# The third query chunk of the first tile moved ahead of the first expert sum on TensorE, and the fourth put beside the first four picks

## Chip, cores and metric

One NeuronCore of a Trainium2 chip runs the whole program. The metric is device time in microseconds, lower is better. All data are float32.

## What is computed

Two transformer blocks on 256 tokens of width 2048. The first block mixes by attention and retention and then applies a layer with 16384 experts, of which each token picks 16 for each of 8 heads. The part that matters here, cut from the reference:

```python
def peer(x, w_query, sub_keys, expert_down, expert_up):
    qry = (xt @ w_query).reshape(T, H, 2, PEER_HALF_DIM)          # 2048 -> 2048
    s = jnp.einsum('thpd,phnd->thpn', qry, sub_keys)               # scores of the keys
    top_s, top_i = lax.top_k(s, K)
    ...
    best_s, best_pos = lax.top_k(cand_s.reshape(T, H, K * K), K)
    expert_idx = jnp.take_along_axis(cand_i.reshape(T, H, K * K), best_pos, axis=-1)
    gates = jax.nn.softmax(best_s, axis=-1)
    ...
        u = expert_down[ib]                                        # 128 experts of each token
        act = jax.nn.gelu(jnp.einsum('td,thkd->thk', xb, u), approximate=False)
        vv = expert_up[ib]
        return jnp.einsum('thk,thkd->td', gb * act, vv)
```

The second block has forgetting attention, a recurrent branch, and 32 dense experts in four groups.

## The kernel before

The tokens are two tiles of 128 (`T2 = 2`). The first tile goes ahead: its projections, attention, retention and output product run alone up to about 500 us. Then the expert layer of the first block begins, in **picks**: `n` of 0 to 127 is the first tile, 128 to 255 the second, and pick `n` is the n-th chosen expert of each of the 128 tokens. For each pick

- GpSimd issues two indirect gathers, in program order: the down row of 128 tokens (128 x 2048 f32, 1 MB) into a ring of three places (`DOWN_ROWS`), freed by the dot product of pick n-3, and the up row of the same size into a ring of three places, four from pick 12 on, freed when its earlier row has been added. The fourth place for the first tile is `XT[:, 0]`, the first tile's turned activations; it is free when the last unit of the fourth query chunk has been used (L881);
- VectorE takes the dot product of the down row with the normed activations (L2561);
- ScalarE applies gelu and gate, and writes a diagonal matrix (L1937 to L1945);
- TensorE adds the up row by four matmuls with that diagonal (L1497, the "sum" of the pick) into banks 0 to 3. Where `n % 4 == 3` VectorE adds it instead (L2412), after the dot product of pick n+1.

The indices come from `choose(g)` on VectorE, 32 picks at a time. `choose(g)` needs the key scores of head pair g, that is chunk g of the query product. `choose(0)` runs whole before pick 0; `choose(1)` is spread over picks 0 on, `choose(2)` over 32 on, `choose(3)` over 64 on, and `choose(4)`, the first of the second tile, starts at the pick `FIFTH`.

The query product of the first tile has four chunks of 512 columns. Chunk `c` is four **units** (`query_unit(c, j)`, two for chunk 0), each with a weight load of its own and 4 matmuls of 128 x 512 (L946). A chunk goes to bank 4 or 5 in turn, is kept by ScalarE (`keep_query`), turned (L952), kept, and multiplied with the keys (`key_scores`, L1068).

Weights are loaded by SyncE in a fixed order of units. From the second query chunk on a unit is 1 MB and lies in a ring of four places; a load waits until the unit four ahead of it has been used.

Beside the picks run the rest of the second tile's first block (units `in1` for its projections, then `gate_a`, `gate_r`, `att`, `ret`, `mix`, `query`), and from pick 129 on the second block of the first tile. `steps_beside_picks()` writes this order by hand: tables with **ticks**, one tick for each pick, and for each engine which steps come after that pick's own work. Each engine runs its table in order. The first lines build the query steps and set the tick `at = x + 4` from which all the second tile's steps follow; the second block's starts are constants (134 and 261).

Of the kernel before, what the change touches and what calls it, by code (L numbers as in the profile page):

```python
# [131 lines left out]
def steps_beside_picks():  # L132

    pe, act, dve = {}, {}, {}

    def put(table, tick, *step):
        table.setdefault(tick, []).append(step)

    when = {}
    for i in range(8):  # L140
        key = ("query", 0, 2 + i // 4, i % 4)
        when[key] = int(i * 1.15)
        put(pe, when[key], *key)
    for c in (2, 3):
        x = when["query", 0, c, 3]
        put(act, x + 1, "query", 0, c)
# [200 lines left out]
def two_blocks(nc, A, consts, out):  # L347
    f32, u32 = mybir.dt.float32, mybir.dt.uint32
    ALU, ACT, AX = mybir.AluOpType, mybir.ActivationFunctionType, mybir.AxisListType.X
    AFTER1 = steps_of_first_block()  # L350
    BESIDE_PE, BESIDE_ACT, BESIDE_DVE, FIFTH, TICKS = steps_beside_picks()
    ds = bass.ds

    ctx = ExitStack()
    with ctx:
# [218 lines left out]
        def slot(i, n=CH):  # L574

            _, lo, hi = PLACES[i]
            return W[:, :, :].rearrange("p s n -> p (s n)")[:, lo:hi].rearrange("p (k n) -> p k n", n=n)

        def depth(key):

            _, lo, hi = PLACES[INDEX[key]]
            return (hi - lo) // columns(key)
# [67 lines left out]
        def query_out(t, c):  # L650

            return bank[4 + (c if t else c % 2)]
# [5 lines left out]
        def keys_out(t, c):  # L658

            return bank[4 + c if t else 7]  # L660
# [247 lines left out]
        def _(pe):  # L908
            turns = 0

            def xt(k, t):
                return XT[:, t, k * P:(k + 1) * P]
# [27 lines left out]
            def unit(key, out, lhs, first, last):  # L940

                i = INDEX[key]
                pe.wait_ge(w_loaded[SLOT[i]], LANDED[i])
                ks = depth(key)
                for k in range(ks):
                    mm = pe.matmul(out, lhs(k), slot(i)[:, k, :], start=first and k == 0, stop=last and k == ks - 1)  # L946
                mm.then_inc(w_used, 1)
# [91 lines left out]
            def query_unit(c, j):  # L1039

                if j == 0 and c >= 2:
                    pe.wait_ge(query_kept, c - 1)
                elif j == 0:
                    pe.wait_ge(mixed, 4)
                    pe.wait_ge(merged_kept, 4)
                if c == 0:
                    pe.wait_ge(kept1, 2 + 2 * j)
                ks = 4 if c else 8
                unit(("query", 0, c, j), query_out(0, c)[:, :], lambda k: xt(ks * j + k, 0), j == 0, ks * j + ks == KC)

            def turn_query(t, c):

                pe.wait_ge(query_kept, 4 * t + c + 1)
                if t == 0 and c:
                    pe.wait_ge(qt_kept, c)
                elif t == 0:
                    pe.wait_ge(kept1, 4)
                turn_four(qt_out(t, c), QN[:, c % 2, :]).then_inc(query_turned, 1)

            def key_scores(t, c):  # L1060

                pe.wait_ge(qt_kept, 4 * t + c + 1)
                pe.wait_ge(keys_kept, 4)
                if t == 0 and c:
                    pe.wait_ge(s_kept, c)
                for j in range(4):
                    b = 4 * c + j
                    mm = pe.matmul(keys_out(t, c)[:, j * P:(j + 1) * P], QT[:, c % 2, j * P:(j + 1) * P],  # L1068
                                   KT[:, (b % 2) * 8 + b // 2, :], start=True, stop=True)
                mm.then_inc(peer_scored, 1)  # L1070
# [281 lines left out]
            for c in range(2):  # L1352
                for j in range(4 if c else 2):
                    query_unit(c, j)
                turn_query(0, c)
                key_scores(0, c)

            def turn2(t, c):

                pe.wait_ge(x2_ready, t + 1)  # L1360
                if t == 1:
                    pe.wait_ge(out2_added, 4)
                    pe.wait_ge(attn_kept, 6)
                turn_four(bank[c], H[:, t, c * CH:(c + 1) * CH]).then_inc(turned2, 1)
# [303 lines left out]
        def _(act):  # L1668
# [84 lines left out]
            def exps(n):  # L1753
                _, _, _, _, sm, _ = att(n)
                _, _, nk = group(n)
                act.wait_ge(scores_ready, n + 1)
                for hh in range(4):
                    act.activation(sm[:, hh, 0:nk], sm[:, hh, 0:nk], ACT.Exp, bias=nmx[:, hh:hh + 1],
                                   accum_out=rs[:, hh:hh + 1]).then_inc(exp_ready, 1)
                if n < 4:  # L1760
                    act.activation(es, es, ACT.Exp).then_inc(exp_ready, 1)
                else:
                    act.activation(es, nmx, ACT.Copy).then_inc(exp_ready, 1)
# [1103 lines left out]
```

## Time and profile before

| | |
|---|---|
| median of 3 runs | 3296.32 us (3295.13 to 3297.55) |
| profiled execution, time | 3301.08 us |
| profiled execution, span | 3299.3 us |
| TensorE busy | 2946.0 us (89%) |
| VectorE busy | 1237.3 us (38%) |
| ScalarE busy | 545.2 us (17%) |
| GpSimd busy | 705.8 us (21%) |
| moved by DMA | 1206.78 MB, mean 366 GB/s |

The time of the profiled execution is 1.8 us above its span. Busy time is a sum over stages that differ in what limits them; the rows below keep them apart.

### The profile page before, as it was taken

How to read it: one execution, taken by the hardware profiler on the slowest of the kernel's cores; microseconds unless marked ns; L12 is line 12 of the kernel's file. 1: busy time of each engine (PE TensorE's matmuls, PEld its weight loads, DVE VectorE, ACT ScalarE, POOL GpSimd, SP SyncE). 2: the span in 40 equal slices, each digit the busy share in tenths (PEclk: the TensorE clock that was granted, in tenths of full speed). 3: DMA queues.
4: the chain of work that ended last, by engine and by line, in shares of the span. 5: the costliest groups of instructions: out<-in, count | busy, mean ns of one | idle time of the engine just before them, and what ended most of it. 6: DMA issues, size and time to landing. Idle time of an engine off the chain costs nothing.

```text
span 3299.3 us, 23959 instructions
## 1 busy us (share of the span) xinstructions
PE 2946.0 (89%) x8013; PEld 1300.7 (39%) x8013; DVE 1237.3 (38%) x1894; ACT 545.2 (17%) x1292; POOL 705.8 (21%) x598
## 2 busy tenths in 40 slices
PE   8999998799889999897687877877799999999999
PEld 4444443344444434343333333333254433333344
DVE  1100005535354443335755655554522123322220
ACT  1111001112121110112213211211122111001010
POOL 1000002323233222324534443434300000000000
PEclk9999999999999999998898989898899999999999
DMA  9878887999999999999999999999977759999972
GB/s 352 300 279 289 301 301 295 417 412 410 412 374 417 421 422 421 421 421 417 408 419 372 417 418 419 419 419 420 374 249 259 259 208 422 422 422 422 422 302 76
DMA packets 268049, 1206.78 MB, mean 366 GB/s; under 512 B 16640, under 2 KB 19248, under 8 KB 164656
## 3 DMA queue, kind: packets, MB, share of 16 engines
q1 hardware_dynamic: 193600, 668.09, 52.4%
q0 software_dynamic: 74352, 537.48, 39.6%
q8 instruction: 51, 0.84, 0.1%
q14 instruction: 46, 0.38, 0.0%
HBM read 1203.41 MB, written 2.10 MB: 365 GB/s over the span
## 4 chain that ended last, share of the span: by engine, by line
PE 46%; DMA 40%; DVE 4%; issue 4%; DVEq 2%; ACT 2%; POOL 1%; SPq 1%; ACTq 0%; POOLq 0%
DMA W<-in_peer_expert_down,big 26%; PE bank L946 14%; DMA W<-in_w_expert_up 8%; PE bank L936 6%; PE bank L1497 6%; PE bank L1108 5%; PE bank L1604 4%; PE bank L1662 3%; DMA W<-in_w_in 3%; DVE W L2561 2%; DVEq L2411 1%; DMA XT<-in_peer_expert_up,big 1%; PE bank L1013 1%; PE bank L1372 1%; DMA W<-in_w_peer_query 1%
## 5 line engine op out<-in xcount | busy, mean ns | idle before, releaser
L2561 DVE CUSTOM_DVE_ANT_0 W<-W,big 128x2048 f32<-128x2048 f32 x256 | 586.1, 2291 | 695.8 <-DMA W<-in_peer_expert_down,big 694.5
L874 POOL DMA_INDIRECT W<-in_peer_expert_down,big x256 | 349.2, 1364 | 1228.0 <-DVE small L2561 629.1
L1497 PE MATMUL bank<-XT,big 128*128 128x512 f32 x488 | 300.3, 773 | 205.2 <-ACT big L1945 178.6
L946 PE MATMUL bank<-W,XT 128*128 128x512 f32 x704 | 308.6, 596 | 3.3 <-DMA W<-in_w_peer_query 3.3
L1497 PE MATMUL bank<-XS,big 128*128 128x512 f32 x536 | 249.8, 610 | 34.0 <-ACT big L1945 26.4
L1497 PEld LDWEIGHTS bank<-XT,big 128*128 128x128 f32 x488 | 119.2, 254 | 374.4 <-issue 244.4
L1497 PE MATMUL bank<-W,big 128*128 128x512 f32 x512 | 238.1, 609 | 26.9 <-ACT big L1945 21.1
L1937 ACT ACTIVATE small<-small 128x1 f32<-128x1 f32 x256 | 51.8, 202 | 1227.6 <-DVE small L2561 1222.0
L1604 PE MATMUL bank<-W,XS 128*64 128x512 f32 x1024 | 226.7, 596 | 14.3 <-DMA W<-in_w_expert_up 11.7
L1108 PE MATMUL bank<-W,XT 128*128 128x512 f32 x480 | 217.1, 602 | 21.3 <-DMA W<-in_w_in 19.1
L936 PE MATMUL bank<-W,XT 128*128 128x512 f32 x480 | 211.9, 599 | 3.0 <-DMA W<-in_w_in 3.0
L946 PEld LDWEIGHTS bank<-W,XT 128*128 128x128 f32 x704 | 133.5, 191 | 166.3 <-issue 161.2
L883 POOL DMA_INDIRECT XS<-in_peer_expert_up,big x130 | 163.0, 1254 | 161.3 <-PE bank L1497 121.2
L946 PE MATMUL bank<-W,big 128*128 128x512 f32 x448 | 194.4, 593 | 1.0 <-ACT big L1725 1.0
L1013 PE MATMUL bank<-W,XT 128*128 128x512 f32 x384 | 170.0, 597 | 2.0 <-DVE XT L2093 2.0
L1497 PEld LDWEIGHTS bank<-XS,big 128*128 128x128 f32 x536 | 101.1, 194 | 172.4 <-issue 149.5
L1497 PEld LDWEIGHTS bank<-W,big 128*128 128x128 f32 x512 | 98.5, 196 | 151.8 <-issue 143.5
L899 POOL COPY XS<-XT 128x448 f32 x32 | 17.0, 561 | 654.5 <-issue 369.8
L2412 DVE SCALAR_TENSOR_TENSOR H<-XS,small,H 128x2048 f32<-128x2048 f32 x63 | 148.1, 2351 | 12.3 <-ACT small L1939 6.6
L1108 PEld LDWEIGHTS bank<-W,XT 128*128 128x128 f32 x480 | 90.9, 192 | 138.5 <-issue 110.4
L1372 PE MATMUL bank<-W,XT 128*128 128x512 f32 x320 | 143.8, 592 | 0.0
L1604 PEld LDWEIGHTS bank<-W,XS 128*64 128x64 f32 x1024 | 78.7, 138 | 159.8 <-issue 159.8
(376 smaller groups left out, 2690.9 us busy)
## 6 DMA issues: line engine op xcount, KB each, us to landing
W<-in_w_in SPq DMA_DIRECT2D x66, 2048.0 KB
W<-in_w_in SPq DMA_DIRECT2D x132, 1024.0 KB
W<-in_w_expert_gate SPq DMA_DIRECT2D x68, 1024.0 KB, 15.0
W<-in_w_expert_up SPq DMA_DIRECT2D x68, 1024.0 KB, 17.0
big<-in_w_expert_down SPq DMA_DIRECT2D x32, 2048.0 KB, 12.6
W<-in_w_out SPq DMA_DIRECT2D x16, 2048.0 KB
W<-in_w_out SPq DMA_DIRECT2D x32, 1024.0 KB
W<-in_w_peer_query SPq DMA_DIRECT2D x28, 1024.0 KB
```

Of the source, the lines that this page charges most:

```text
L874: pool.indirect_dma_start(down_row(n), None, down_t, row).then_inc(down_in[n % DOWN_ROWS], 16)
L883: pool.indirect_dma_start(up_row(n), None, up_t, row).then_inc(up_in[b], 16)
L936: mm = pe.matmul(bank[q % 4][:, :], xt(8 * half + k, 0), slot(u)[:, k, :], start=half == 0 and k == 0, stop=half == 1 and k == 7)
L946: mm = pe.matmul(out, lhs(k), slot(i)[:, k, :], start=first and k == 0, stop=last and k == ks - 1)
L1013: mm = pe.matmul(bank[4 + c][:, :], lhs, slot(i, D)[:, 0, c * CH:(c + 1) * CH], start=first, stop=last)
L1108: mm = pe.matmul(bank[4 + c][:, :], xt(ks * j + k, 1), slot(i, width)[:, k, c * CH:(c + 1) * CH], start=j == 0 and k == 0, stop=ks * j + k ...
L1372: mm = pe.matmul(bank[c][:, :], lhs(k), slot(i, 1024)[:, k, c * CH:(c + 1) * CH], start=first and k == 0, stop=last and k == 1)
L1497: mm = pe.matmul(bank[4 * (n // P) + c][:, :], DIAG[:, m % 4, :], up_row(n)[:, c * CH:(c + 1) * CH], start=n % P == 0, stop=n % P == P - 2)
L1604: mm = pe.matmul(bank[2][lo:hi, :], XTE[:, p, 8 * half + k, lo:hi], moving(half, e, k), start=half == 0 and k == 0, stop=half == 1 and k == 7)
L1662: mm = pe.matmul(bank[2 * (n % 2) + t][:, :], xt(8 * j + k, t), slot(u)[:, k, :], start=j == 0 and k == 0, stop=j == 1 and k == 7)
L2412: STT(h, up_row(n), wts[:, j:j + 1], h, ALU.mult, ALU.add).then_inc(added_dve, 1)
L2561: dve.tensor_tensor_reduce(out=down_row(n), in0=down_row(n), in1=HN[n // P], scale=1.0, scalar=0.0, op0=ALU.mult, op1=ALU.add, accum_out=d ...
```

## The change

The query units of the third chunk (`c = 2`) are written ahead of the loop over the picks, right behind the key scores of the second chunk, so they precede the first sum. The units of the fourth chunk (`c = 3`) go to ticks 0, 1, 2 and 3. Before, the eight units had the ticks 0, 1, 2, 3, 4, 5, 6 and 8.

```diff
     when = {}
-    for i in range(8):
-        key = ("query", 0, 2 + i // 4, i % 4)
-        when[key] = int(i * 1.15)
-        put(pe, when[key], *key)
+    for j in range(4):
+        when["query", 0, 2, j] = -1
+        when["query", 0, 3, j] = j
+        put(pe, j, "query", 0, 3, j)
     for c in (2, 3):
         x = when["query", 0, c, 3]
         put(act, x + 1, "query", 0, c)
...
                 turn_query(0, c)
                 key_scores(0, c)
+            for j in range(4):
+                query_unit(2, j)
```

The loop below takes its ticks from `x`. The third chunk's keep, turn and key scores move from ticks 4 to 7 to ticks 0 to 3, the fourth's from 9 to 12 to 4 to 7. `at` becomes 7 instead of 12, and with it every step of the second tile's first block stands 5 ticks earlier, and `FIFTH` is 111 instead of 116. The order of SyncE's loads and of GpSimd's gathers is the same.

TensorE's order of before, from the second query chunk to the fifth sum. L946 from `W,XT` is query units (4 matmuls each), L952 turning, L1068 key scores, L1497 the sum of a pick:

```order
L946 MATMUL bank<-W,XT 128x512 x16
L952 MATMUL bank<-C,big 128x128 x4
L1068 MATMUL bank<-big 128x128 x4
L1497 MATMUL bank<-W,big 128x512 x4
L946 MATMUL bank<-W,XT 128x512 x4
L1497 MATMUL bank<-XS,big 128x512 x4
L946 MATMUL bank<-W,XT 128x512 x4
L1497 MATMUL bank<-XS,big 128x512 x4
L946 MATMUL bank<-W,XT 128x512 x8
L1497 MATMUL bank<-XS,big 128x512 x4
L946 MATMUL bank<-W,XT 128x512 x4
L1497 MATMUL bank<-XS,big 128x512 x4
```

The same place with the change (the sum's line is now L1499):

```order
L946 MATMUL bank<-W,XT 128x512 x16
L952 MATMUL bank<-C,big 128x128 x4
L1068 MATMUL bank<-big 128x128 x4
L946 MATMUL bank<-W,XT 128x512 x16
L1499 MATMUL bank<-W,big 128x512 x4
L946 MATMUL bank<-W,XT 128x512 x4
L1499 MATMUL bank<-XS,big 128x512 x4
L946 MATMUL bank<-W,XT 128x512 x4
L952 MATMUL bank<-C,big 128x128 x4
L1499 MATMUL bank<-XS,big 128x512 x4
L946 MATMUL bank<-W,XT 128x512 x4
L1068 MATMUL bank<-big 128x128 x4
```

Sixteen matmuls have gone from between the sums to a place ahead of the first.

VectorE's order of before at the normalization of the second tile's retention. L2561 is a pick's dot product (the second row of each pair reads out its sum), L2412 an addition of an up row, L2217 to L2226 the normalization, L2400 and L2402 the end of `choose(2)`:

```order
L2561 ISA W,small<-W,big 128x2048
L2561 ISA small 128x1
L2400 RECIPROCAL small<-small 128x2
L2402 TENSOR_TENSOR big<-big,small 128x32
L2561 ISA W,small<-W,big 128x2048
L2561 ISA small 128x1
L2217 RECIPROCAL small<-small 128x8
L2222 TENSOR_SCALAR big<-big,small 128x256 x8
L2226 TENSOR_TENSOR big<-big 128x2048
L2561 ISA W,small<-W,big 128x2048
L2561 ISA small 128x1
L2412 SCALAR_TENSOR_TENSOR H<-XS,small,H 128x2048
```

The same with the change (line numbers two higher):

```order
L2563 ISA W,small<-W,big 128x2048
L2563 ISA small 128x1
L2386 TENSOR_TENSOR big<-big,C 128x512
L2219 RECIPROCAL small<-small 128x8
L2224 TENSOR_SCALAR big<-big,small 128x256 x8
L2228 TENSOR_TENSOR big<-big 128x2048
L2563 ISA W,small<-W,big 128x2048
L2563 ISA small 128x1
L2389 TENSOR_TENSOR big<-big 128x512
L2563 ISA W,small<-W,big 128x2048
L2563 ISA small 128x1
L2414 SCALAR_TENSOR_TENSOR H<-XS,small,H 128x2048
```

The normalization now stands between steps of `choose(2)`, and one more dot product lies between it and the next addition.

## Rows read from the trace of the kernel before

**Rows 1.** The page: span, bus rate in 40 slices, chain by engine.

```profile
span 3299.3 us, 23959 instructions
...
GB/s 352 300 279 289 301 301 295 417 412 410 412 374 417 421 422 421 421 421 417 408 419 372 417 418 419 419 419 420 374 249 259 259 208 422 422 422 422 422 302 76
...
PE 46%; DMA 40%; DVE 4%; issue 4%; DVEq 2%; ACT 2%; POOL 1%; SPq 1%; ACTq 0%; POOLq 0%
```

**Rows 2.** Busy time by stage, granted clock, DMA share, rate.

```profile
core 0: us, PE busy (x) PEld busy (x) DVE busy (x) ACT busy (x) POOL busy (x), PEclk, DMA share, GB/s
...
530.00:1500.00 970.00, 878.68 (x2126) 395.46 (x2127) 415.93 (x543) 158.98 (x419) 291.12 (x230) 0.96 1.01 412
1500.00:2380.00 880.00, 676.21 (x1525) 297.67 (x1524) 519.43 (x693) 198.22 (x531) 366.93 (x282) 0.88 1.01 413
```

**Rows 3.** Timeline of TensorE: start, duration, group [idle time before it, releaser].

```profile
514.02 13.90 PE L946 MATMUL bank<-W,XT 128*128 128x512 f32 x32
...
529.95 1.16 PE L1068 MATMUL bank<-big 128*128 128x128 f32 x8 [0.69 <-ACT big L1865]
542.74 6.46 PE L1497 MATMUL bank<-W,big 128*128 128x512 f32 x8 [11.64 <-ACT big L1945]
549.05 3.60 PE L946 MATMUL bank<-W,XT 128*128 128x512 f32 x8
552.48 3.60 PE L1497 MATMUL bank<-XS,big 128*128 128x512 f32 x8
...
600.73 3.70 PE L946 MATMUL bank<-W,XT 128*128 128x512 f32 x8 [1.93 <-DMA W<-in_w_peer_query]
```

**Rows 4.** Timeline of VectorE: the indices, the first dot product.

```profile
531.20 0.19 DVE L2393 SCALAR_TENSOR_TENSOR big<-big 128x32 uint32<-128x32 f32 x1
...
537.89 2.29 DVE L2561 CUSTOM_DVE_ANT_0 W<-W,big 128x2048 f32<-128x2048 f32 x1 [3.80 <-DMA W<-in_peer_expert_down,big]
```

**Rows 5.** Timeline of GpSimd: the first gather, the seventh and the eighth.

```profile
532.41 1.04 POOL L874 DMA_INDIRECT W<-in_peer_expert_down,big  x1 [453.95 <-issue]
...
541.30 0.94 POOL L874 DMA_INDIRECT W<-in_peer_expert_down,big  x1 [0.30 <-issue]
550.02 2.77 POOL L883 DMA_INDIRECT W<-in_peer_expert_up,big  x1 [7.79 <-PE bank L1497]
```

**Rows 6.** Slices of 2 us, columns as in rows 2.

```profile
532.00:534.00 2.00, 0.00 (x0) 0.00 (x0) 0.45 (x3) 1.36 (x2) 1.28 (x2) 1.00 0.18 70
534.00:536.00 2.00, 0.00 (x0) 0.00 (x0) 0.09 (x1) 0.00 (x0) 1.67 (x2) 0.68 0.91 262
536.00:538.00 2.00, 0.00 (x0) 0.00 (x0) 0.11 (x1) 0.00 (x0) 1.41 (x2) 0.50 0.97 377
...
552.00:554.00 2.00, 2.00 (x6) 0.95 (x5) 1.14 (x8) 0.90 (x3) 1.70 (x2) 1.00 0.83 217
554.00:556.00 2.00, 2.00 (x6) 0.85 (x5) 1.35 (x1) 0.00 (x0) 0.03 (x1) 1.00 0.79 307
```

**Rows 7.** A slice of a stretch with gathers alone.

```profile
1580.00:1600.00 20.00, 11.88 (x24) 4.78 (x23) 10.56 (x12) 2.50 (x9) 8.97 (x8) 0.83 1.01 420
```

**Rows 8.** Timeline of VectorE: its wait for the inner products.

```profile
906.26 0.69 DVE L2200 TENSOR_TENSOR big<-bank,C 128x512 f32<-128x512 f32 x1 [25.86 <-PE bank L1141]
```

**Rows 9.** Slices of 20 us, columns as in rows 2.

```profile
900.00:920.00 20.00, 20.00 (x54) 9.44 (x53) 6.30 (x9) 4.19 (x8) 5.68 (x4) 1.00 0.85 317
920.00:940.00 20.00, 17.79 (x50) 9.18 (x49) 12.56 (x14) 7.50 (x15) 8.74 (x4) 1.00 0.91 361
...
980.00:1000.00 20.00, 11.20 (x29) 5.30 (x29) 14.98 (x19) 8.83 (x20) 11.72 (x8) 0.83 0.96 365
...
1040.00:1060.00 20.00, 20.00 (x48) 8.93 (x47) 4.60 (x4) 1.80 (x6) 2.81 (x3) 1.00 1.02 423
...
1800.00:1820.00 20.00, 15.24 (x31) 6.66 (x32) 19.31 (x43) 6.79 (x14) 9.88 (x6) 0.83 0.77 287
```

**Rows 10.** The dot products: duration min/median/max, first and last start.

```profile
L2561 DVE CUSTOM_DVE_ANT_0 W<-W,big x256: 2258/2292/2348, 537.9 to 2383.8; 128x2048 f32<-128x2048 f32 x128
```

## The prediction

> **What bounds the kernel now.** I read the page first, then the stage table, the timeline around the first pick on TensorE, VectorE and GpSimd, the same stretch in slices of 2 us, and the places where the DMA engines were not full.
>
> The page [rows 1] shows where TensorE and the DMA engines meet: in the chain, TensorE has 46% and DMA 40%, and the rate on the bus jumps from about 300 GB/s to above 410 in the eighth slice, where the picks begin. The stage table [rows 2] gives the split. From 530 to 1500 us (picks 0 to about 111, with the second tile's weights beside them) the DMA moved 412 GB/s, its share reads 1.01, while TensorE was busy 878.68 of 970 us, 91%. From 1500 to 2380 us it is the same with TensorE at 676.21 of 880. After 2380 us no pick is left, and the change does not touch that part. So the stretch in which the change acts runs at the rate of the DMA engines. TensorE comes second, close behind: it has 9% of slack up to 1500 us.
>
> Around the first pick [rows 3] the reader is to see one hole. TensorE ends the key scores of the second query chunk at 531.1 us and starts the first sum at 542.74, 11.64 us later. The chain across that hole is serial [rows 4, 5]: VectorE writes the indices at 531.20, GpSimd issues the first gather at 532.41, the first dot product starts at 537.89, ScalarE makes the diagonal, and TensorE sums. And the first sum is slow: 6.46 us for the same four matmuls that take 3.60 a few us later [rows 3]. The granted clock in 534 to 536 us is 0.68 [rows 6], and 0.50, the 1.2 GHz level, in the slice behind it.
>
> **What the change does to TensorE at the hole.** It puts the four units of the third query chunk (16 matmuls) where TensorE was idle. The second chunk, the same 16 matmuls, took 13.90 us [rows 3]. From 531.1 us that ends at 545.0, which is 2.3 us after the old start of the first sum. But TensorE has then not been idle, so I take the sum at 3.60 us instead of 6.46: it ends at 548.6 instead of 549.2. So the first sum ends no later, and 13.9 us of matmuls are already done. If TensorE set the pace afterwards, the change would be worth 13.9 + 0.6 = 14.5 us. The cost of this edit on the first picks is thus about nothing. If the clock stayed at the lower level the sum would end at 545.0 + 6.46 = 551.5 us, 2.3 us late; the cover for this is that the next gather into the up ring waits for that sum [rows 5], and the seven gathers ahead of it are 7.3 MB, 17.6 us at full rate from about 534 us, so the engines are fed until then.
>
> The Trainium skill, TensorE: Matmul & The Clock Gate (Part 1: The HAM clock gate), says the same of the mechanism: the default is the throttled clock, and activity releases it. By it too the first sum would run at full clock; the sum is the same without it.
>
> **What it does to the DMA engines.** The bytes are the same, in the same order in SyncE's queue. What can be gained is time in which the engines now lie idle and would have something to load. The units live in a ring of four places of 1 MB, so the loads of the fourth chunk wait for the units of the third to be used. Before, the first of these is used up at 552.6 us [rows 3]; now, at 3.5 us a unit, at 534.6, 538.1, 541.5 and 545.0. So four loads of 1 MB are asked for 18 us or more earlier. From 532 to 556 us [rows 6] the slices that fall short of the 418 GB/s of a full one are:
> - 532 to 534 us, 70 GB/s: too early, the first new load is asked for at 534.6 us. Gain nothing.
> - 534 to 536 us, 262 GB/s: the gathers are just starting. The missing (418-262)/418 x 2 = 0.7 us may be half filled. 0.4 us.
> - 552 to 554 us, 217 GB/s and 554 to 556 us, 307 GB/s: GpSimd waited 7.79 us until 550.02 with the fourth up gather, and in program order the next down gather stands behind it [rows 5]. A weight load fills this now: (201+111)/418 x 2 = 1.5 us.
> Together 1.9 us. Elsewhere the new loads only take bandwidth from gathers that the same engines carry. The second and third down rows land later, by up to 4.2 MB / 418 GB/s = 10 us, and this is given back when those bytes are no longer due. The 13.9 us that TensorE has won turns into waits for rows and weights.
>
> The Trainium skill, DMA: Bandwidth & Descriptors (Issuing engines are not separate DMA queues), states the rule that speaks against a larger gain: transfers of SyncE and GpSimd run on the same 16 engines and interleave. [rows 2] with 1.01 at 412 GB/s agree with it. By it the 14.5 us are not to be had while the engines are full.
>
> **What moves with it.** The third chunk no longer takes ticks 0 to 3, the fourth takes 0 to 3 instead of 4 to 8, and the table derives every later step of the second tile from that. So turns, key scores, all `in1` units, attention, retention and the six wide products stand 5 picks earlier, beside GpSimd's queue, which is unchanged; SyncE's queue is in the same order too. The steps of the second block (from tick 129) stay. So five gather-only picks move from ahead of the `in1` units to behind the last query unit. A gather-only stretch is at full rate too, 420 GB/s at 1580 to 1600 us [rows 7]: cost nothing. The first gather into the place freed by the fourth chunk's last unit (pick 12) comes after it with more room. The other 3 up places have to do for picks 7 to 11 beside two units each; by count, a pick there moves 4.2 MB, 10 us, so the ring covers 30 us. A row needs some 14 of them: 5.5 from the issue to the dot product, 2.3 for that, 2.6 for the diagonal, 3.6 for the sum [rows 3 to 5]. Nothing.
>
> What I can't price is the alignment. Of four picks, one is added by VectorE, not TensorE, and its addition stands behind the next dot product. A shift by 5 moves every step by one against that pattern, and against VectorE's choosing of the next indices (ticks 32 to 50). That matters where VectorE, in order, waits for TensorE: at 906.26 us it had waited 25.86 us for the inner products [rows 8], and queued behind that are the dot products, for which the down gathers wait. DMA then fell to 317 and 361 GB/s at 900 to 940 us and to 365 at 980 to 1000 [rows 9], against 423 in full flow. By 418 GB/s that is 4.8, 2.7 and 2.5 us, 10.0 in all, in the steps from the first inner products to the normalization. Bounds: all of it goes (-10.0), or as much again is added (+10.0). The same waits exist after as before, with three of their four TensorE ticks holding a sum in both. I take 0.
>
> **The sum.** The profiled execution has a span of 3299.3 us and a time of 3301.08. 3301.08 - 1.9 = 3299.2. The median of the runs is 4.76 us below the profiled execution, so on their scale 3296.32 - 1.9 = 3294.4 us. I take 3294.5.
>
> **The rivals.**
> - TensorE sets the pace. For it: TensorE at 20.00 us of 20 at 1040 to 1060 [rows 9], and 91% over the stretch. Against it: in the same row the DMA engines are full. All 14.5 us would give 3281.8. It needs the DMA engines to find 14 us of idle time up to tick 50; there are the 1.9 and the 10.0.
> - The shift, with TensorE 13.9 us ahead, closes the holes at 900 to 1000 us. 1.9 + 10.0 = 11.9 us: 3284.4. Half of it, 6.9 us, is at the edge of what can be told. For it: the normalization now stands one dot product away from VectorE's addition instead of right ahead of it. Against: TensorE's lead is spent at the start, since it waits there for the same bytes.
> - A new hole, slower. One VectorE wait of the attention or retention falls together with an addition or a choosing step, the down gathers stop, and four weight places can't keep the engines full. How deep such a hole can be shows 1800 to 1820 us, 287 GB/s, which is 6.3 us lost [rows 9]; with a repeat as at 900 to 940 it is 10. Then 3294.4 + 10.0 = 3304.4. It decides (slower by over 0.2%) once new holes exceed 6.6 + 1.9 = 8.5 us.
> - The change does nothing: the third chunk's own loads are late and TensorE waits all the same. The load of its last unit can start when the second chunk's last unit is used up, at 527.9 us [rows 3]; 1 MB at full rate is 2.5 us, and even at twice that it is there before 541.5, when TensorE comes to it. I give this no separate time; it is within the forecast.
>
> **How the numbers follow.** A measurement of this kernel tells 0.2%, 6.6 us, from no change. Forecast (3294.4, with alignment within +-5 us): 0.55. Holes closed, by more than half: 0.24. TensorE's pace: 0.05. New holes: 0.16, of which some 0.12 pass the bound. Faster by over 0.2%: 0.24 + 0.05 less a little that falls short, 0.27. Slower: 0.12 and 0.03 for what I haven't thought of, 0.15. Same: 0.58. The range is to leave 2 in 10 out: from the closed holes (3284.4) with 1 us to spare, to just below the new hole's end, 3303. TensorE's pace lies outside. The forecast's own range is 3289 to 3300.
>
> **What would show each step.** Right: no idle time of 11 us ahead of the first sum, its four matmuls in 3.6 us, its end near 548.6 us; the slices at 552 to 556 us full; the fourth chunk's last unit done near 570 us instead of 604 [rows 3]; the picks' last dot product (now 2383.8 us by its start [rows 10]) earlier by only about 2 us. Wrong: a last dot product earlier by over 7 us, with the slices at 900 to 1000 us near 418 GB/s; or a new row of under 350 GB/s between 600 and 1000 us, and VectorE waiting over 20 us for TensorE beside it.

## The result, and the profile after

The changed kernel takes 3304.55 us (median, 3300.32 to 3307.93) against 3296.42 for the kernel before on the same chip (3293.69 to 3299.04): ratio 1.0021, 95% interval [1.0012, 1.0029]. It is slower, and above the range, whose upper end was 3303. The ratio here and below is the record's estimate from all single runs with its interval; it is not the quotient of the two medians, which would be 1.0025. In microseconds the loss is 6.9 [4.0, 9.6] by the ratio and 8.1 by the medians.

The page of the changed kernel (span, bus rate in 40 slices, chain by engine), which answers to [rows 1]:

```profile
span 3302.5 us, 23959 instructions
...
GB/s 353 302 275 293 301 295 307 414 382 402 415 387 422 421 421 421 421 421 414 420 419 360 417 419 419 418 419 419 376 238 268 261 205 422 421 422 422 422 304 76
...
PE 48%; DMA 38%; DVE 4%; issue 4%; DVEq 3%; ACT 1%; SPq 1%; POOL 1%; ACTq 0%; POOLq 0%
```

The eighth slice, where the picks begin, is 414 against 417; the ninth (660 to 743 us) has fallen from 412 to 382, and the tenth (743 to 826 us) from 410 to 402. Start and end of the dot products, as [rows 10]:

```profile
L2563 DVE CUSTOM_DVE_ANT_0 W<-W,big x256: 2258/2292/2327, 537.5 to 2386.4; 128x2048 f32<-128x2048 f32 x128
```

The picks end 2.6 us later than in [rows 10], although the execution profiled there was 4.8 us above its median and this one lies on it. So the two traces show 2.6 us of a loss of 7 to 8, and I read places from them, not the sum.

TensorE at the first sums (columns as in [rows 3]):

```profile
530.39 13.90 PE L946 MATMUL bank<-W,XT 128*128 128x512 f32 x32
544.12 3.60 PE L1499 MATMUL bank<-W,big 128*128 128x512 f32 x8
550.79 3.67 PE L946 MATMUL bank<-W,XT 128*128 128x512 f32 x8 [3.07 <-DMA W<-in_w_peer_query]
554.30 3.60 PE L1499 MATMUL bank<-XS,big 128*128 128x512 f32 x8
562.76 5.40 PE L946 MATMUL bank<-W,XT 128*128 128x512 f32 x8 [4.87 <-DMA W<-in_w_peer_query]
...
576.20 3.60 PE L946 MATMUL bank<-W,XT 128*128 128x512 f32 x8
```

The idle 11.64 us are filled, the first sum takes 3.60 us and ends at 547.7. The third chunk did what it was to do. The slices (columns as in [rows 2]):

```profile
552.00:554.00 2.00, 2.00 (x6) 0.89 (x5) 1.91 (x4) 0.20 (x1) 0.00 (x0) 1.00 1.01 410
554.00:556.00 2.00, 2.00 (x6) 0.82 (x5) 0.97 (x7) 0.70 (x2) 0.00 (x0) 1.00 1.02 413
640.00:660.00 20.00, 10.37 (x15) 4.24 (x16) 7.57 (x9) 0.90 (x3) 2.98 (x1) 0.74 1.03 405
660.00:680.00 20.00, 20.00 (x48) 8.92 (x47) 6.68 (x11) 1.48 (x4) 5.91 (x4) 1.00 0.90 333
680.00:700.00 20.00, 20.00 (x55) 9.37 (x55) 8.10 (x10) 4.22 (x14) 6.05 (x4) 1.00 0.97 368
780.00:800.00 20.00, 20.00 (x59) 9.77 (x58) 8.48 (x11) 3.34 (x10) 3.30 (x3) 1.00 0.90 357
```

The two slices of [rows 6] that fell short are full. But there is a new hole at 660 to 700 us, and a smaller one at 780 to 800 us (357, where the kernel before has 417), to which the section on the units comes back. Of the first, the order is the thing to see: from 640 to 660 the DMA engines are full and TensorE works 10.37 us of 20; then TensorE works 20.00 of 20 and the DMA engines fall to 333. Each in turn waits for the other. TensorE ahead of the hole:

```profile
623.90 3.60 PE L1499 MATMUL bank<-XS,big 128*128 128x512 f32 x8
627.34 3.60 PE L1108 MATMUL bank<-W,XT 128*128 128x512 f32 x8
632.69 3.70 PE L1108 MATMUL bank<-W,XT 128*128 128x512 f32 x8 [1.76 <-DMA W<-in_w_in]
644.63 5.64 PE L1108 MATMUL bank<-W,XT 128*128 128x512 f32 x8 [8.24 <-DMA W<-in_w_in]
655.27 5.40 PE L1108 MATMUL bank<-W,XT 128*128 128x512 f32 x8 [5.00 <-DMA W<-in_w_in]
660.50 3.60 PE L1499 MATMUL bank<-XT,big 128*128 128x512 f32 x8
```

VectorE and GpSimd behind it:

```profile
671.79 0.29 DVE L2120 TENSOR_TENSOR big<-big,C 128x128 f32<-128x128 f32 x1 [23.93 <-ACT big L1745]
```

```profile
664.91 0.94 POOL L883 DMA_INDIRECT XT<-in_peer_expert_up,big  x1 [17.03 <-PE bank L1499]
675.21 1.35 POOL L883 DMA_INDIRECT W<-in_peer_expert_up,big  x1 [8.12 <-PE bank L1499]
```

The rows at 644.63 and 655.27 are units 8 and 9 of `in1`, the first two of group 1 (keys and values of the second tile's attention). TensorE waited 8.24 and 5.00 us for their weights. Pick 11 has no sum on TensorE, so the sum of pick 12 stands behind both, at 660.50, and GpSimd, in program order, gathered nothing for 17.03 us.

### The profile page after: what moved, and what is told of

It is laid out like the page before. It is cut to its first block, busy times and chain, and to the rows that moved or that the text cites. A ratio compares the mean times of both kernels' runs of the same rounds, so it can differ in the third digit from the quotient of the medians.

```text
span 3302.5 us, 23959 instructions
## 1 busy us (share of the span) xinstructions
PE 2953.6 (89%) x8013; PEld 1304.5 (40%) x8013; DVE 1236.1 (37%) x1894; ACT 545.0 (17%) x1292; POOL 709.4 (21%) x598
## 4 chain that ended last, share of the span: by engine, by line
PE 48%; DMA 38%; DVE 4%; issue 4%; DVEq 3%; ACT 1%; SPq 1%; POOL 1%; ACTq 0%; POOLq 0%
DMA W<-in_peer_expert_down,big 26%; PE bank L946 14%; DMA W<-in_w_expert_up 8%; PE bank L1499 7%; PE bank L936 5%; PE bank L1108 5%; PE bank L1606 4%; PE bank L1664 3%; DMA W<-in_w_in 3%; DVEq L2413 2%; PE bank L1013 1%; DVE W L2563 1%; PE bank L1374 1%; PE bank L1590 1%; DMA XT<-in_peer_expert_up,big 1%
## 5 line engine op out<-in xcount | busy, mean ns | idle before, releaser
L1499 PE MATMUL bank<-XT,big 128*128 128x512 f32 x488 | 312.7, 800 | 210.8 <-ACT big L1947 177.3
L946 PE MATMUL bank<-W,XT 128*128 128x512 f32 x704 | 309.9, 598 | 7.9 <-DMA W<-in_w_peer_query 7.9
L1499 PEld LDWEIGHTS bank<-XT,big 128*128 128x128 f32 x488 | 122.4, 261 | 385.1 <-issue 278.1
L1499 PE MATMUL bank<-XS,big 128*128 128x512 f32 x536 | 244.6, 600 | 23.9 <-ACT big L1947 21.2
L1499 PE MATMUL bank<-W,big 128*128 128x512 f32 x512 | 236.6, 606 | 22.1 <-DMA W<-in_peer_expert_up,big 13.2
L1606 PE MATMUL bank<-W,XS 128*64 128x512 f32 x1024 | 225.4, 593 | 14.1 <-DMA W<-in_w_expert_up 11.5
L946 PEld LDWEIGHTS bank<-W,XT 128*128 128x128 f32 x704 | 133.9, 192 | 171.0 <-issue 164.6
L946 PE MATMUL bank<-W,big 128*128 128x512 f32 x448 | 194.4, 593 | 1.0 <-ACT big L1727 1.0
L1499 PEld LDWEIGHTS bank<-XS,big 128*128 128x128 f32 x536 | 99.2, 191 | 154.4 <-issue 140.9
L1499 PEld LDWEIGHTS bank<-W,big 128*128 128x128 f32 x512 | 98.3, 194 | 149.2 <-issue 129.2
## 6 DMA issues: line engine op xcount, KB each, us to landing
W<-in_w_out SPq DMA_DIRECT2D x32, 1024.0 KB, 11.5
```

What stands on the lines that cost most here:

```text
L1499: mm = pe.matmul(bank[4 * (n // P) + c][:, :], DIAG[:, m % 4, :], up_row(n)[:, c * CH:(c + 1) * CH], start=n % P == 0, stop=n % P == P - 2)
L1606: mm = pe.matmul(bank[2][lo:hi, :], XTE[:, p, 8 * half + k, lo:hi], moving(half, e, k), start=half == 0 and k == 0, stop=half == 1 and k == 7)
```

## What the experiments tell apart

All ratios are to the kernel before, run on the same chip as the experiment (its median was 3297.37, 3298.62, 3297.85, 3297.65 and 3298.99 us in the five sets), five rounds each, and hold 95% intervals. Where a run is "the changed kernel with", the rest is as in the diff.

### The query chunks, or the shift

Two theories. *Chunks*: the earlier query loads beside the first gathers cost. *Shift*: the second tile's steps at tick 7 in place of 12 cost.

```diff
-    at = x + 4
+    at = 12        # e1;  at = 8 in e2
```

> Both query chunks as in the change (third ahead of the first sum, fourth at ticks 0 to 3), but every later step of the second tile back at its old tick (at = 12 instead of 7). Theory shift: the loss comes from the second tile's steps standing 5 ticks earlier; then this is level with the kernel before or up to 2 us faster, ratio 0.9990 to 1.0005. Rival chunks: the loss comes from the query weights that are loaded beside the first gathers; then this is as slow as the change, ratio about 1.002.

e1: 3298.96 us, 1.0003 [0.9994, 1.0012].

> The change with the second tile's steps moved by 4 ticks instead of 5 (at = 8), so that every step stands at the old place in the pattern of four picks. Theory parity (a kind of shift): the place among the four picks decides; then this is within 2 us of the kernel before. Theory ring: what costs is units of the second tile beside picks that still have three up places (before pick 12); then this is slow like the change, ratio about 1.002.

e2: 3297.59 us, 1.0002 [0.9993, 1.0011].

In e4 the third chunk alone goes ahead of the first sum, and the fourth has the ticks 4, 5, 6 and 8, so that nothing is shifted:

> Only the third chunk goes ahead of the first sum; the fourth stays at ticks 4, 5, 6 and 8 and the second tile's steps stay where they were (at = 12). Theory shift: level or up to 2 us faster, ratio 0.9990 to 1.0005. Rival chunks: slower, about half or all of the loss, ratio 1.001 to 1.002.

e4: 3296.82 us, 0.9997 [0.9988, 1.0006].

*Chunks* falls: without the shift, one chunk moved (e4) or both (e1) make no difference that can be told. The loss belongs to the shift. But a shift of four ticks (e2) costs nothing and one of five 2.1 thousandths, so it is not how early the steps are. The ticks between, `at = 9` (e6), `10` (e8) and `11` (e5):

> The second tile's steps moved by 3 ticks (at = 9). Theory parity (only a start one tick ahead of a multiple of four is bad): level, 0.9995 to 1.0005. Rival early: level too. A ratio over 1.001 speaks against both.

> The second tile's steps moved by 2 ticks (at = 10). Theory parity: level, 0.9995 to 1.0005. Rival early: level. With the other starts this completes the scan from 7 to 12.

> The change with the second tile's steps moved by 1 tick instead of 5 (at = 11, which has the same remainder by 4 as the change's 7). Theory parity: a hole of 5 to 7 us at the first two rotations as in the change, ratio about 1.0015. Rival early: only the start at 7 is too early, and this is level with the kernel before, 0.9995 to 1.0005.

Measured: 1.0000 [0.9991, 1.0009] at 9 (3298.80), 1.0025 [1.0014, 1.0035] at 10 (3307.47), 1.0025 [1.0016, 1.0034] at 11 (3307.73). Tick 11 came as *parity* had it. Tick 10 did not: level was expected, by both theories, so a start one tick ahead of a multiple of four is not the only bad one.

### The place against VectorE's picks

VectorE adds the picks with remainder 3 by 4. If the distance from these counts, then moving the pattern must undo the loss of the changed kernel (e9), and can bring one on the kernel before (e10):

```diff
-BY_DVE = [n for n in range(PICKS) if n % 4 == 3]
-BY_PE = [n for n in range(PICKS) if n % 4 != 3]
+BY_DVE = [n for n in range(PICKS) if n % 4 == (2 if n < 60 else 3)]   # 1 in e10
+BY_PE = [n for n in range(PICKS) if n not in BY_DVE]
```

> The change as it is, with all ticks kept, but for picks below 60 VectorE adds those with remainder 2 by 4 instead of 3. The four narrow units (the 512 key and value columns, 2 KB rows) stand at ticks 11 and 12; the pick without a sum on TensorE is then 10 instead of 11. Theory pattern: a narrow unit on a tick without a sum is what costs; back to the kernel before, ratio 0.9990 to 1.0007, hole at 620 to 700 us under 3 us. Rival place: the absolute tick of the steps decides (against the choosing of indices, or the up ring); still 1.0015 to 1.0025.

Measured 3294.73, 0.9989 [0.9980, 0.9998], the lowest ratio of all.

> The kernel before with no part of the change; for picks below 60 VectorE adds those with remainder 1 instead of 3. Its narrow units stand at ticks 16 and 17, and pick 17 is now without a sum on TensorE. Theory pattern: slower than before, ratio 1.001 to 1.0025, with a hole of 4 us or more at 640 to 720 us. Rival place: level, 0.9995 to 1.0005.

Measured 3301.72, 1.0010 [0.9999, 1.0020]: in the direction expected, at the edge of the interval. The control, remainder 2 on the kernel before:

> The kernel before with VectorE adding picks 2, 6, 10 ... 58 in place of 3, 7, 11 ... 59; the second tile's steps stay at tick 12. Theory 'distance to VectorE's picks': the steps' start less the remainder is 10, 2 by modulo 4, one of the level distances, so 0.999 to 1.000 (3296). If remainder 2 is better by itself, whatever the distance, then this is as fast as the changed kernel with it: 0.999 or below.

Measured 3296.48, 0.9998 [0.9989, 1.0007]. The table is by distance (tick of the second tile's first unit less the remainder, modulo 4). It has TensorE's waits for all `in1` weights from 590 to 700 us and the mean rate from 530 to 1020 us. "Narrow pair" is the time in which the 1024 pieces of 2 KB of units 8 and 9 were moved, counted by size from the packets of each trace. The next column is the lowest of the three slices of 20 us from 780 to 840 us. Both are taken up below.

| kernel | tick, remainder | distance | waits, us | GB/s | narrow pair, us | lowest, 780 to 840 | ratio |
|---|---|---|---|---|---|---|---|
| before | 12, 3 | 1 | 5.9 | 403 | 11.5 | 412 | 1 |
| e1 | 12, 3 | 1 | 5.1 | 403 | 10.3 | 413 | 1.0003 |
| e4 | 12, 3 | 1 | 4.9 | 406 | 13.0 | 414 | 0.9997 |
| e2 | 8, 3 | 1 | 6.0 | 405 | 10.5 | 410 | 1.0002 |
| e9 | 7, 2 | 1 | 9.9 | 407 | 13.0 | 415 | 0.9989 |
| e6 | 9, 3 | 2 | 8.3 | 406 | 12.1 | 394 | 1.0000 |
| e16 | 12, 2 | 2 | 6.6 | 409 | 10.2 | 392 | 0.9998 |
| e8 | 10, 3 | 3 | 11.4 | 396 | 13.5 | 265 | 1.0025 |
| e10 | 12, 1 | 3 | 7.5 | 402 | 12.1 | 335 | 1.0010 |
| after | 7, 3 | 0 | 15.0 | 400 | 19.5 | 357 | 1.0021 |
| e5 | 11, 3 | 0 | 15.2 | 399 | 22.3 | 374 | 1.0025 |

The rule by distance was written down in this form only ahead of e16. e9's own expectation was narrower: a narrow unit on a tick without a sum on TensorE costs. At distance 0 units 8 and 9 stand on such a tick (11 in the changed kernel, 15 at tick 11). At distance 1 it is units 6 and 7, whose pieces are wide, and most of the waits of the table are for these. (So of the waits that e17's expectation gives for the kernel before, 2.08 and 3.48 us are for units 6 and 7; only 0.33 is for a narrow one. The 1.44 us of e18's is also for unit 7.)

### What makes the hole: the ring, the hold, the order

A "hold" is VectorE standing, in program order, at a step that waits for another engine, with dot products behind it.

The fourth up place from pick 8 in place of 12:

```diff
-        spare = [3] if 12 <= n < P else [4] if n >= P else []
+        spare = [3] if 8 <= n < P else [4] if n >= P else []
```

> The change with the fourth up place used from pick 8 instead of pick 12 (it is free once the fourth chunk's last unit is used, at tick 3). Theory ring: back to the kernel before or 2 us faster, ratio 0.999 to 1.0005, and the slices at 660 to 700 us full. Theory parity, or one in which VectorE's waits for ScalarE and TensorE at the rotations stop the down gathers: no change, ratio about 1.002.

Measured 3302.89, 1.0015 [1.0006, 1.0024]; the two slices of the hole rise from 333 and 368 to 366 and 386 GB/s. At most a part: 1.0015 and 1.0021 are not told apart.

The second rotation one pick later, so that VectorE does not stand in front of it:

```diff
-    put(dve, last[1] + 2, "rope1", 1)
-    put(pe, x + 5, "turn_in1", 2, KA, 6)
-    put(act, x + 6, "turn_in1", 2, KA, 6)
+    put(dve, last[1] + 3, "rope1", 1)
+    put(pe, x + 6, "turn_in1", 2, KA, 6)
+    put(act, x + 7, "turn_in1", 2, KA, 6)
```

> The change with one step of VectorE one tick later: the second rotation (rotate the two key heads, tick 14 to 15), and the turning behind it on TensorE and ScalarE one tick later. Theory hold: in the change VectorE stands 23.9 us at that rotation while the down gathers wait for its dot products; one more dot product ahead of it feeds the gathers, the hole of 7.3 us at 620 to 700 us shrinks to under 4, ratio 1.0005 to 1.0015. Rival: the hole comes from TensorE's late weights, and the ratio stays at 1.002.

Measured 3305.67, 1.0021 [1.0012, 1.0030]. VectorE's wait falls from 23.93 only to 20.17 us and the slice from 660 us stays at 333. One more dot product ahead of the wait does not help; the trace has GpSimd standing for a sum (17.03 us in the changed kernel, 16.59 here), not for a dot product. So this wait does not start the hole at 660 us. The edit left most of the wait in place, so what it would be worth without it is not shown.

The sum of pick 12 ahead of units 8 and 9, in the changed kernel (e11) and with `at = 11` (e12, there the sum of pick 16):

```diff
-        when[key] = at + i // 2 if i < 12 else int(at + 6 + (i - 12) * 0.625)
+        when[key] = at + (i // 2 if i not in (8, 9) else 5) if i < 12 else int(at + 6 + (i - 12) * 0.625)
```

> The change with two units moved by one tick: the first two narrow units from tick 11 (no sum) to tick 12, so that TensorE does the sum of pick 12 ahead of them. Theory narrow units: the sum ends some 20 us earlier, the up gather behind it goes out, and the hole at 620 to 700 us shrinks from 7.3 to under 3 us; ratio 1.0000 to 1.0012. Rival hold: VectorE still waits over 20 us at the second rotation, and the ratio stays at 1.002.

> The start at 11 (ratio 1.0025) with the same two units one tick later, from tick 15 (no sum) to 16. Theory narrow units: the hole at 620 to 700 us shrinks from 4.8 to under 2.5 us and the ratio falls to 1.0005 to 1.0015. Rival hold: no change.

Measured 3305.20 both, 1.0020 [1.0011, 1.0029] and 1.0020 [1.0010, 1.0029]. The edit did its work and won nothing that can be told, and the narrow form of the theory falls with it: in e11 that sum comes at 639.79 in place of 660.50, but the next one is now the one behind the late units, and GpSimd stands for it:

```profile
639.79 5.20 PE L1499 MATMUL bank<-XT,big 128*128 128x512 f32 x8 [2.37 <-ACT big L1947]
671.53 3.60 PE L1499 MATMUL bank<-W,big 128*128 128x512 f32 x8
```

```profile
675.93 1.34 POOL L883 DMA_INDIRECT W<-in_peer_expert_up,big  x1 [24.56 <-PE bank L1499]
```

So what remains to explain is why the units are late.

### Why the units are late: the pieces of their loads

The DMA queues of the changed kernel while TensorE waits for unit 8 (packets, MB, share of the 16 engines; q0 is the gathers, q1 the weights):

```profile
DMA packets 1075, 4.96 MB, mean 414 GB/s; under 512 B 79, under 2 KB 79, under 8 KB 599
...
q0 software_dynamic: 538, 3.90, 78.6%
q1 hardware_dynamic: 537, 1.07, 23.6%
```

From 632 to 644 us both queues had work and each moved the same number of packets, 538 and 537. A gather's packet is 3.90 MB / 538 = 7.2 KB in the mean (476 rows of 8 KB and 62 records of 4 bytes), a weight's 1.07 / 537 = 2.0 KB: the units of group 1 are 512 columns wide, the others 1024. So the weights get 1.07 MB in 12 us, and a unit of 1 MB takes some 12 us: the 11.9 between 632.69 and 644.63. The other units' pieces are twice as long. To test that, the group's four loads are read as 1024 columns of half as many row blocks:

```diff
+                if ORDER[i][:3] == ("in1", 1, 1):
+                    k = 2 * ORDER[i][-1]
+                    wide = A["w_in"][0].rearrange("(k p) n -> p k n", p=P)[:, k:k + 2, KA:KA + 1024]
+                    sp.dma_start(slot(i, 1024), wide).then_inc(w_loaded[SLOT[i]], 16)
+                    return
```

> The changed kernel, but the four narrow weight units of the second tile (keys and values of its attention, 512 columns each, read in pieces of 2 KB) are read as 1024 columns of half as many row blocks: the same 1 MB each, into the same place, in pieces of 4 KB. The second tile's attention keys and values are therefore computed from other weights, so its picks are other experts. Theory 'narrow pieces' (the narrow loads get less than their share beside the gathers' 8 KB rows, TensorE waits for them at 644 to 660 us, and the sum and the gathers behind follow late): TensorE's waits for these weights (8.24 and 5.00 us) fall below 4 us, the slices at 660 to 700 us (333 and 368 GB/s) come above 400, and the ratio falls to about 1.000 (3298). Theory 'place of the steps' (it is the order of sums and steps, whatever the loads look like): holes and ratio stay, 1.002 (3305).

Measured 3301.77, 1.0009 [1.0000, 1.0019]. The queues in the same 12 us, and then TensorE (its lines are five higher):

```profile
q0 software_dynamic: 451, 3.28, 65.6%
q1 hardware_dynamic: 447, 1.75, 36.5%
```

```profile
631.23 3.70 PE L1113 MATMUL bank<-W,XT 128*128 128x512 f32 x8 [0.32 <-DMA W<-in_w_in]
638.42 5.40 PE L1113 MATMUL bank<-W,XT 128*128 128x512 f32 x8 [3.50 <-DMA W<-in_w_in]
645.64 3.70 PE L1113 MATMUL bank<-W,XT 128*128 128x512 f32 x8 [1.82 <-DMA W<-in_w_in]
649.18 3.60 PE L1504 MATMUL bank<-XT,big 128*128 128x512 f32 x8
```

The second tile's keys and values are computed from other weights here, so its picks are other experts: the kernel computes something else and serves for its times alone. Still packet for packet, 451 to 447, but the weights now get 1.75 MB; the units come 7.2 us apart and the sum 11.3 us earlier. Each wait is below 4 us, as *narrow pieces* had it; the slices at 660 to 700 us come to 390 and 393, not above 400, and the ratio halfway. So the pieces carry part of it. The control on the kernel before, and the repeat on `at = 11`:

> Control for the wide pieces: the kernel before, with the four narrow weight units read as 1024 columns of half as many row blocks (4 KB pieces, the same bytes; the second tile's attention keys and values are computed from other weights, so its picks are other experts). Before, TensorE waited only 2.08, 3.48 and 0.33 us for these units and no hole followed. Theory 'narrow pieces are the cause of the loss': nothing to win here, 0.9995 to 1.0005. If the other experts of the second tile, or less DMA time of the wide pieces, make any kernel faster: 0.999, and the 1.2 thousandths that the changed kernel won by it are not its own.

Measured 3296.91, 0.9996 [0.9987, 1.0004].

> The same wide pieces in the other slow kernel, the one with the second tile's steps at tick 11 (1.0025, TensorE waited 1.44, 9.04 and 4.77 us for the narrow units); the second tile's attention keys and values are computed from other weights here too. Theory 'narrow pieces': the waits fall to 4 us or below, the slices at 680 to 700 us fill, and the ratio falls by about as much as in the changed kernel, to 1.0010 to 1.0015. If the changed kernel's gain was chance: 1.0025.

Measured 3301.34, 1.0007 [0.9998, 1.0016], from 1.0025. The gain is 1.2 of 2.1 thousandths in the changed kernel, 1.8 of 2.5 at tick 11, and 0.4 [-0.4, 1.3] where there was no hole. Each interval is about 0.9 wide on either side. So at tick 11 the gain is clear of nothing, in the changed kernel (1.2, give or take 1.3) just not; that it is larger than where there was no hole is likely and not shown.

Why the kernels at the good distances are spared by the same narrow loads is in the queues too. At `at = 8`, from 644 to 655 us, while its narrow units are loaded:

```profile
q1 hardware_dynamic: 1144, 2.26, 55.2%
q0 software_dynamic: 305, 2.15, 47.5%
```

The gathers thinned out and then paused, and the weights took 1144 packets. The column "narrow pair" of the table shows it for all kernels: at distance 0 the pieces of units 8 and 9 take 19.5 and 22.3 us, beside 722 and 863 rows of the gathers; in the nine others they take 10.2 to 13.5 us, beside 237 to 412 rows. So at the good distances a pause in the gathers meets the narrow loads, and at distance 0 it comes when they are nearly through. In the changed kernel that is 655 to 666 us:

```profile
DMA packets 1289, 3.57 MB, mean 325 GB/s; under 512 B 64, under 2 KB 64, under 8 KB 1288
...
q1 hardware_dynamic: 1288, 3.56, 87.7%
```

There is no q0 here at all: GpSimd waits for the sum behind the late units, the weights' ring fills, and the engines run dry. At distance 3 the narrow pair is no slower than in e9 (13.5 and 12.1 us against 13.0), so these two kernels need another explanation.

### The units alone

TensorE's `in1` units one pick later, as at tick 8, all that follows them as in the change:

```diff
-        put(pe, when[key], *key)
+        put(pe, when[key] + 1, *key)
```

> The changed kernel, with only TensorE's weight units of the second tile's projections one pick later (where they stand when all steps start at tick 8), and all that follows them (keeps, rotations, turns, attention, retention, on every engine) where the change puts it. Theory 'units' (what costs is where the weight units stand against the sums that TensorE does and leaves out): as with all steps at tick 8, level, 1.000 to 1.0005 (3298), with 660 to 700 us above 400 GB/s. Theory 'VectorE's steps' (what costs is where the rotations, additions and softmax steps stand against the dot products and additions on VectorE): unchanged, 1.002 (3305), with the waits of 23 us on VectorE.

Measured 3306.58, 1.0026 [1.0016, 1.0036]. *Units* fails, and *VectorE's steps* has the number but not with the hole that it meant: the waits for `in1` weights are 5.8 us here, as in a good kernel. VectorE now stands at the first rotation, one dot product ahead of where it stands at tick 8 (there it waits 19.22 us, after one more down gather has gone out). The dot products queue behind it and the gathers behind these. (The gather's row names TensorE, but by the code a down gather waits for a dot product; the one behind the rotation, from 657.60 us, ended in the same moment as the sum.)

```profile
653.54 0.69 DVE L2120 TENSOR_TENSOR big<-big,C 128x512 f32<-128x512 f32 x1 [24.40 <-ACT big L1745]
```

```profile
660.70 2.98 POOL L874 DMA_INDIRECT W<-in_peer_expert_down,big  x1 [27.34 <-PE bank L1499]
```

```profile
655.00:665.00 10.00, 10.00 (x21) 4.25 (x20) 8.37 (x10) 0.90 (x3) 3.92 (x2) 0.83 0.38 122
```

122 GB/s for 10 us. This is the second kind of hole, the hold of [rows 8], and e8 (26.54 us at 811.78, 265 GB/s at 800 to 820) and e10 have it as well, at the scores of the second tile's attention. e10, with 338 GB/s at 800 to 820 us beside it:

```profile
815.03 1.29 DVE L2159 SCALAR_TENSOR_TENSOR big<-bank,C 128x512 f32<-128x512 f32 x2 [26.30 <-PE bank L1198]
```

The changed kernel has it too, at the same step, with 357 GB/s at 780 to 800 us: the dot products stand behind the scores, and the next down gather behind these. The same step in the changed kernel, in the kernel before and in e13:

```profile
791.19 1.29 DVE L2161 SCALAR_TENSOR_TENSOR big<-bank,C 128x512 f32<-128x512 f32 x2 [24.15 <-PE bank L1198]
797.33 2.21 POOL L874 DMA_INDIRECT W<-in_peer_expert_down,big  x1 [9.65 <-DVE small L2563]
```

```profile
810.35 1.29 DVE L2159 SCALAR_TENSOR_TENSOR big<-bank,C 128x512 f32<-128x512 f32 x2 [22.44 <-PE bank L1198]
```

```profile
788.43 1.29 DVE L2166 SCALAR_TENSOR_TENSOR big<-bank,C 128x512 f32<-128x512 f32 x2 [25.22 <-PE bank L1203]
```

Over the kernels of the table, this wait is 24.15 to 26.54 us at distances 3 and 0, and the lowest slice from 780 to 840 us is 265 to 374 GB/s; at distances 1 and 2 it is 11.96 to 22.44 us, and no slice is below 392. e3, e11 and e12, which stayed slow, have 23.26 to 23.38 us and 371 to 387. With wide pieces this hole is still there, and deeper: 331 GB/s in e13, and 316 (wait 25.78) in e18, where the first hole is gone (no slice from 660 to 760 us below 407). So the slow kernels of distance 0 have two holes. At 418 GB/s they are 7.1 us (640 to 700) and 2.9 us (780 to 800) in the changed kernel's trace, and the wide pieces fill only the first. No run takes the second away alone. Why a wait of 24.15 us opens it and one of 22.44, with the same 10 us for which GpSimd stands, does not, is not shown.

### The best version

e9 with the ring of e3:

> The changed kernel with VectorE adding picks 2, 6, 10 ... 58 in place of 3, 7, 11 ... 59 (alone that gave 0.9989) and with the fourth place of the up ring open from pick 8 in place of 12 (alone that took 0.6 thousandths off). If the two gains are of different causes they add: 0.998 to 0.9985 (3292). If the ring only helped because of the hole that the pattern has closed: 0.999 as without it (3294).

Measured 3296.29, 0.9991 [0.9982, 1.0000]. That is level with e9; the sum of the two gains, 0.998 to 0.9985, lies at the edge of the interval. So the ring most likely helped only because of the hole. e9 has the lowest ratio, 3.1 us below before by the medians on its chip.

## Why the prediction was wrong

- **The idle time at the first sum, its duration, the 1.9 us.** Right, but for the 1.9 us, which the runs can't tell from nothing. The sum ends at 547.7 (forecast 548.6), both slices are full, and TensorE's 13.9 us won nothing: 3.07 and 4.87 us of them went at once in waits for weights. The edit without its shift is e1, +1.0 [-2.0, 4.0] us; the forecast of -1.9 is at the edge of that (e4, -1.0 [-4.0, 2.0], holds it well). The fourth chunk ends at 579.8 and not near 570; 7.9 us of that are the two waits for weights, whose loads share the engines with the gathers.
- **TensorE sets the pace.** Did not happen, for the reason given.
- **The failed step is "What I can't price is the alignment ... I take 0."** The term was bounded at +-10 us, and it measures +5.9 to +7.9 by the ratios: the changed kernel's 6.9 us less what the chunks do without the shift, +1.0 us in e1 and -1.0 in e4 (by the medians +6.5 to +8.7). That is inside its bounds; taking 0 for it is what failed. The reason for 0 was "The same waits exist after as before, with three of their four TensorE ticks holding a sum in both". That counted sums for VectorE's waits at 900 us. The larger hole that came is at 660 us, behind waits for weights, which the term did not look at; the second, at 780 us, is at a wait of VectorE of the kind that it had in view, at an earlier step.
- **The rival that came true is "A new hole, slower".** 3304.4 was its time; that the median came within 0.2 us of it is luck, as its 10.0 us was the depth of other holes. Its mechanism is half right. It fits the hole at 780 us, where VectorE waits 24.15 us and the down gather behind it 9.65. At 660 us VectorE also waits over 20 us (23.93), but e7 and GpSimd's row say that the hole does not start there: it starts with TensorE waiting for weights of narrow pieces.
- **"A pick there moves 4.2 MB, 10 us, so the ring covers 30 us."** Wrong in kind: bytes do not share the engines, packets do. By bytes units 8 and 9 were due every 5 us beside two gathers; they came after 11.9 and 10.6. And the "Nothing" behind it used 5.5 us from issue to dot product, read where the engines were empty [rows 5, 6]; beside the weights, from 632 to 644 us, the gathers landed 16.7 to 17.2 us after their issue.
- **The price of a hole.** "Closed holes", 10.0 us to win, came in part and was outweighed: 900 to 920 us is at 391 now, but 940 to 980 us is at 365 and 370. At 418 GB/s, 900 to 1000 us is short by 6.2 us in the changed kernel's trace and by 10.4 in that of before.

Open stays what the hole at the scores costs by itself, and whether it is the whole of what is left when the pieces are wide, 0.9 [0.0, 1.9] thousandths; and how much of the loss at tick 10 is of each kind. There the sum of pick 16 stands behind the narrow units 10 and 11 (348 GB/s at 680 to 700 us), and the scores follow with 265. The distance rule is read from eleven kernels; that e10 is slower by it is not certain, and only e16 was run after the rule was written down. No run tried the narrow loads ahead of the burst, as it needs another place for them.

## What to carry to other kernels

When a hand-written order is shifted against a periodic one, price the alignment as a term of its own: run the shift at each of its residues (here four kernels) before judging the edit that caused it. Where two DMA queues are busy, compute a load's time from its packets, not its bytes: next to 8 KB rows, a load in 2 KB pieces gets a fifth of the rate. And look for slices in which first one resource is full and then the other; a bus that is full at that moment says nothing about who gets it.

## What the runs showed of the hardware

With both queues busy the engines took packets one for one, whatever their size: 538 to 537 with 2.0 KB pieces of weights, 451 to 447 with pieces twice as long, 494 to 493 at tick 11 (655 to 666 us), and beside the 4 KB pieces of the ordinary units 295 to 296 in the changed kernel from 612 to 620 us. The Trainium skill, DMA: Bandwidth & Descriptors (Queues, rings and completion order), says that each engine goes round the queues that have work, a packet at a time; the traces agree, and add that the turn is blind to size. The page's packet is a bundle of descriptors, and no run here shows that what the profile counts as a packet is the same. The total hardly suffers, 414 GB/s against 419 with wide pieces; the share of the weights does, 1.07 MB against 1.75 in 12 us.
